# Six output parts, squares added by VectorE and other unused matmuls in a two-block fp32 kernel

## What is computed

```python
# first block
xn = rms_norm(x, attn_norm_g);  proj = xn @ w_in
x = x + concat(moba_attention(...), gated_linear_attention(...)) @ w_out
hn = rms_norm(x, ffn_norm_g)
h = causal_dwconv(hn @ w_ffn_up, conv_w, conv_b)        # width 3, over tokens
x = x + (silu(h_gate) * h_val) @ w_ffn_down             # d_ff = 2816
x = rms_norm(x, final_norm_g)
# second block: shift, scale and gate of each sublayer come from silu(c) @ w_ada + b_ada
x = x + 0.5 * g1 * swiglu(modulate(rmsnorm(x, ffn1_norm), sh1, sc1), ffn1_w_in, ffn1_w_out)
x = x + g2 * (latent attention, chunk attention, two gates, w_out)(modulate(rmsnorm(x, mix_norm), sh2, sc2))
x = x + 0.5 * g3 * swiglu(modulate(rmsnorm(x, ffn2_norm), sh3, sc3), ffn2_w_in, ffn2_w_out)
return rmsnorm(x, final_norm)
```

## Time and profile before

| | us |
|---|---|
| median of 3 runs | 876.56 |
| lowest, highest | 872.31, 880.18 |
| the profiled execution | 875.95 |
| its span (first to last instruction) | 874.1 |
| TensorE busy in it | 859.3 |

### The profile page before, as it was taken

The page is one execution under the profiler, slowest core; times in us unless marked ns, Lnnn a source line. Parts: engine busy times, 40 slices in busy tenths (PEclk is TensorE's granted clock), DMA queues, the critical chain, the costliest instruction groups (busy, mean ns, idle before and its releaser), DMA issues.

```text
span 874.1 us, 19335 instructions
## 1 busy us (share of the span) xinstructions
PE 859.3 (98%) x7326; PEld 833.8 (95%) x7326; DVE 709.1 (81%) x1109; ACT 477.7 (55%) x747; POOL 101.2 (12%) x134
## 2 busy tenths in 40 slices
PE   7999999999999999999999999999999999999996
PEld 6988899999999999999999999988999999999996
DVE  3898866889999978888889977888889998766552
ACT  4756576555555567444445567565645764444451
POOL 1031102000001540000002301000010200000021
PEclk6999999999999999999999999999999999999998
DMA  7453338566668984788889958655587568555651
GB/s 271 145 164 112 114 118 278 162 193 219 214 219 280 369 284 144 225 295 291 290 291 324 339 162 277 203 187 193 175 280 275 178 202 290 192 192 192 217 169 49
DMA packets 53384, 191.68 MB, mean 219 GB/s; under 512 B 5936, under 2 KB 6464, under 8 KB 53264
## 3 DMA queue, kind: packets, MB, share of 16 engines
q1 hardware_dynamic: 41760, 149.96, 51.3%
q0 software_dynamic: 10704, 39.20, 13.5%
q10 hardware_dynamic: 864, 1.73, 0.6%
HBM read 189.82 MB, written 1.05 MB: 218 GB/s over the span
## 4 chain that ended last, share of the span: by engine, by line
PE 91%; DVE 6%; ACT 1%; issue 1%; DMA 1%; DVEq 0%; SPq 0%; ACTq 0%
PE ps L396 27%; PE ps L397 26%; PE ps L398 26%; DVE w_lo L1320 2%; PE ps L487 1%; PE ps L489 1%; PE ps L488 1%; PE ps L563 1%; PE ps L620 1%; PE ps L509 1%; PE ps L594 1%; DVE ada_raw L1613 1%; DMA X<-x_in 1%; PE ps L580 0%; PE ps L602 0%
## 5 line engine op out<-in xcount | busy, mean ns | idle before, releaser
L1320 DVE TENSOR_TENSOR w_lo<-raw,w_hi 128x1024 fp32r<-128x1024 f32 (+1 forms) x282 | 339.8, 1221 | 76.1 <-ACT w_hi L915 75.3
L396 PE MATMUL ps<-xh,w_hi 128*128 128x256 f32 x1290 | 360.4, 279 | 0.7 <-DVE w_lo L1320 0.6
L397 PE MATMUL ps<-xl,w_hi 128*128 128x256 f32 x1290 | 357.1, 277 | 0.0
L398 PE MATMUL ps<-xh,w_lo 128*128 128x256 f32 x1290 | 357.1, 277 | 0.0
L915 ACT ACTIVATE w_hi<-raw 128x1024 fp32r<-128x1024 f32 (+1 forms) x282 | 288.6, 1050 | 94.2 <-PE ps L398 68.5
L396 PEld LDWEIGHTS ps<-xh,w_hi 128*128 128x128 f32 x1290 | 243.1, 188 | 3.7 <-issue 2.6
L397 PEld LDWEIGHTS ps<-xl,w_hi 128*128 128x128 f32 x1290 | 242.8, 188 | 0.3 <-issue 0.2
L398 PEld LDWEIGHTS ps<-xh,w_lo 128*128 128x128 f32 x1290 | 242.6, 188 | 0.0
L396 PE MATMUL ps<-act_hi,w_hi 128*128 128x256 f32 x528 | 146.6, 278 | 0.4 <-DVE act_lo L1605 0.4
L397 PE MATMUL ps<-act_lo,w_hi 128*128 128x256 f32 x528 | 146.5, 277 | 0.0
L398 PE MATMUL ps<-act_hi,w_lo 128*128 128x256 f32 x528 | 146.5, 277 | 0.0
(11 more groups left out here) (270 smaller groups left out, 1151.8 us busy)
## 6 DMA issues: line engine op xcount, KB each, us to landing
raw<-w SPq DMA_DIRECT2D x282, 512.0 KB, 4.3
ada_raw<-ada_w POOLq DMA_DIRECT2D x72, 512.0 KB, 4.9
X<-x_in SPq DMA_DIRECT2D x4, 256.0 KB, 5.4
out<-X SPq DMA_DIRECT2D x4, 256.0 KB, 2.4
tab<-tab_in ACTq DMA_DIRECT2D x1, 640.0 KB, 4.1
gmask<-gmask_in ACTq DMA_DIRECT2D x1, 512.0 KB, 5.4
cact<-c_in POOLq DMA_DIRECT2D x1, 512.0 KB, 6.5
bm<-bias_in POOLq DMA_DIRECT2D x1, 512.0 KB, 8.3
```

The lines of the kernel that those rows point to most:

```text
L396: pe.matmul(o, lh, rh, start=start, stop=False, skip_group_check=True)
L397: pe.matmul(o, lh, rl, start=False, stop=False, skip_group_check=True)
L398: return pe.matmul(o, ll, rh, start=False, stop=stop, skip_group_check=True)
L1320: v.tensor_tensor(w_lo[:, slot(h), 0:n], raw[:, slot(h), 0:n], w_hi[:, slot(h), 0:n].bitcast(F32), ALU.subtract).then_inc(lo_ready, 1)
```

## The change

- The last products go from four pairs of tiles to six parts (`LAST`: tiles 0, 1, 2 and 3, 4 and 5, 6, 7). SyncE issues the first five transfers, ScalarE the last.
- In the first norm VectorE adds squares: tiles 2 and 3 onto 0 and 1, tiles 4 and 5 onto 0 and 1, tile 7 onto 6. TensorE sums tiles 0, 1 and 6 only.
- In the first norm VectorE no longer does a low part of the weights before the reciprocal. The two low parts stand behind products 0 and 1. ScalarE converts the next weight half before the last group of `xh`.
- Unused matmuls: 6 instead of 4 at the start; 2 instead of 1 at the two entries (`IDLE_ENTRY`); two of 128 columns between sums and spread in each norm by tokens; one of 384 columns before the sums of tile 7 in the last norm.
- `first_two` waits for the first low part only before the first two products, and for the second before the others.
- In the last round of the convolved feed-forward the low part of the weights stands behind the split of the product. In the modulated feed-forwards (`raw_up`) a low part and a split of two tiles change places.

```diff
-IDLE_SPREAD = 1
+LAST = [(0, 1), (1, 1), (2, 2), (4, 2), (6, 1), (7, 1)]
+IDLE_ENTRY = {0: 2, C_UP[0]: 2}
...
-            for p in range(4):
-                sp.wait_ge(resid_done, 5 * KC + 1 + p)
-                sp.dma_start(out[:, 2 * p:2 * p + 2, :], pair(X, p)).then_inc(out_written, 16)
-            sp.wait_ge(out_written, 64)
+            for j, (k, n) in enumerate(LAST[:-1]):
+                sp.wait_ge(resid_done, 5 * KC + 1 + j)
+                sp.dma_start(out[:, k:k + n, :], X[:, k:k + n, :]).then_inc(out_written, 16)
+            sp.wait_ge(out_written, 16 * len(LAST))
...
-            def keep_clock(bank, n):
+            def keep_clock(bank, n, w=3):
                 for _ in range(n):
-                    pe.matmul(ps[:, bank, 0:3 * P], mean[:, 0, :], mean[:, :, :].rearrange("p a n -> p (a n)"), start=True, stop=True)
+                    pe.matmul(ps[:, bank, 0:w * P], mean[:, 0, :], mean[:, 0:w, :].rearrange("p a n -> p (a n)"), start=True, stop=True)
...
             def high_part_first(c, x_wait):
+                pe.wait_ge(lo_ready, 2 * c + 1)
                 pe.wait_ge(xh_ready, x_wait + 1)
                 parts = [(j, f) for j in range(2) for f in range(2)]
                 for j, f in parts:
+                    if j and f == 0:
+                        pe.wait_ge(lo_ready, 2 * c + 2)
...
-                if not shifted:
-                    keep_clock(u % 2, IDLE_SPREAD)
-                pe.wait_ge(lo_ready, h + 2)
-                if not shifted:
+                if shifted:
+                    pe.wait_ge(lo_ready, h + 2)
+                else:
+                    keep_clock(u % 2, IDLE_ENTRY[c])
                     high_part_first(c, x_wait)
...
             def norm_start():
-                for k in range(KC):
-                    if k % 2 == 0:
-                        pe.wait_ge(sq_done, k + 2)
-                    m = token_sums(k, k == 0, k == KC - 1)
+                for j, k in enumerate((0, 1, 6)):
+                    if k != 1:
+                        pe.wait_ge(first_sum, 2 if k == 0 else 3)
+                    m = token_sums(k, j == 0, j == 2)
                 m.then_inc(ss_done, 1)
                 pe.wait_ge(consts_ready, 1)
+                keep_clock(0, 2, 1)
                 norm_spread(0)
-            def norm_tokens(n, q, added, tiles_left):
+            def norm_tokens(n, q, added, tiles_left, c, ahead=0):
+                pe.wait_ge(bank_free[bank_use(c) % 2], bank_use(c) // 2)
                 for j, k in enumerate(tiles_left):
+                    if k == 7:
+                        keep_clock(bank_use(c) % 2, ahead)
...
                 m.then_inc(ss_done, 1)
+                keep_clock(bank_use(c) % 2, 2, 1)
                 norm_spread(n)
...
-            keep_clock(0, IDLE - 2)
+            keep_clock(0, IDLE)
...
-            norm_tokens(1, 1, 2, (6, 0, 1, 7))
+            norm_tokens(1, 1, 2, (6, 0, 1, 7), C_UP[0])
...
-            norm_tokens(6, 5, 24, (0, 7))
+            norm_tokens(6, 5, 24, (0, 7), C_UP[2] + FT, ahead=1)
...
-            def norm_hi(m):
+            def norm_hi(m, weights=None):
                 for j, k in enumerate(NEXT):
+                    if weights is not None and j == len(NEXT) - 1:
+                        hi(weights, halves=(0,))
...
-            norm_hi(0)
-            hi(1)
+            norm_hi(0, weights=1)
+            hi(1, halves=(1,))
...
+            k, n = LAST[-1]
+            act.wait_ge(resid_done, 5 * KC + len(LAST))
+            act.dma_start(out[:, k:k + n, :], X[:, k:k + n, :]).then_inc(out_written, 16)
...
                 rstd_tokens(n)
-                if n == 0:
-                    lo(0, halves=(1,))
                 dve.wait_ge(rstd_spread, n + 1)
                 for j, (k0, n_) in enumerate(NEXT):
...
+                    if n == 0 and j < 2:
+                        lo(0, halves=(j,))
...
-                for p in range(4):
-                    dve.wait_ge(xg_done, 2 * p + 2)
-                    v.tensor_tensor(pair(X, p), pair(xg, p), over(ps[:, 2, 0:S], 2), ALU.mult).then_inc(resid_done, 1)
+                for k, m in LAST:
+                    dve.wait_ge(xg_done, k + m)
+                    v.tensor_tensor(X[:, k:k + m, :], xg[:, k:k + m, :], over(ps[:, 2, 0:S], m), ALU.mult).then_inc(resid_done, 1)
...
-                    if j:
+                    if j and not split_first:
                         lo(c + 2, i=i, halves=(1,))
...
                 v.tensor_tensor(al, av[:, vv, :], ah.bitcast(F32), ALU.subtract).then_inc(act_ready, 1)
+                if split_first:
+                    lo(c + 2, i=i, halves=(1,))
...
-                pair_lo(m, 2)
                 lo(c0 + 4, halves=(0,))
+                pair_lo(m, 2)
...
+            for j, (a, b) in enumerate(((slice(0, 2), slice(2, 4)), (slice(0, 2), slice(4, 6)), (6, 7))):
+                dve.wait_ge(sq_done, 4 + 2 * j)
+                if j == 1:
+                    dve.wait_ge(first_sum, 1)
+                v.tensor_tensor(xn[:, a, :], xn[:, a, :], xn[:, b, :], ALU.add).then_inc(first_sum, 1)
             dve.wait_ge(cols_landed, 16)
-            lo(0, halves=(0,))
             norm_plain(0, 0, "attn_g", 1)
```

More of the change, by code:

```diff
@@ L202, in build @@
         out_written = sem("out_written")
+        first_sum = sem("first_sum")
         block = ctx.enter_context(nc.Block())
@@ L1567, in level_copy, with up_step @@
                         v.copy_predicated(dst, mask, src).then_inc(lv_copied, 1)
-            def up_step(conv, fi, c, j, i=0):
+            def up_step(conv, fi, c, j, i=0, split_first=False):
                 u = bank_use(c)
@@ L1623, in conv_up @@
                         for vv in range(2):
-                            up_step(True, 0, c0 + 2 + vv, 2 + vv, i=i)
+                            up_step(True, 0, c0 + 2 + vv, 2 + vv, i=i, split_first=n is None)
                     if n == 0:
@@ L1666, in raw_up @@
                 raw_av(fi, 1)
+                lo(c0 + 4, halves=(0,))
                 pair_lo(m, 2)
-                lo(c0 + 4, halves=(0,))
                 pair_lo(m, 3)
```

## The result

The changed kernel took 869.26 us (median of 19 runs, 868.26 to 876.60), the kernel before in the same series 874.06 us (median of 19, 870.60 to 880.32). The ratio is 0.9947, with a 95% interval of 0.9926 to 0.9968: a gain of 4.8 us, where 2.5 was forecast, and near the lower end of the range.

A forecast was written before the change was run, and what follows sets the result against it. TensorE, busy 859.3 of 874.1 us, was taken to bound the kernel outside the ends. -2.0 + 0.2 - 0.4 - 0.3 = -2.5 us gave 873.4 from the profiled execution, 874.0 by the median; range 869.0 to 878.5.

The forecast's parts named there:

- The likeliest case: Whole kernel: the forecast's gains and costs come out as summed, giving 872.5 to 875.5 us; chance 0.5.
- Start, -2.0 (0 to -3.0): First norm to gate products: shorter sums and an earlier reciprocal save 2.0 us, with 0 and 3.0 as ends.
- (a): Rival at the start, second norm and end: unused matmuls hold the clock; in all -5.4, 871.2 us; chance 0.2.
- VectorE's chain: Start: root 11.0, first product 13.1 instead of 16.09; 3.0 us won at the front become 1.7 at tile 1.
- Second norm, +0.2 (-1.3 to +0.3): 140 to 147 us: the second wide unused matmul costs 0.2 us; up to 1.3 won if the clock holds.
- Conv feed-forward, -0.4: Last round of the convolved feed-forward's loop: TensorE's stop before 273.46 us goes, saving 0.4 us, between 0.4 and 0.
- End, -0.3 (-0.7 to +0.4): Last products and output: the first transfer starts 0.27 us earlier and the end moves with it, -0.3 us.
- The swap, 0: Modulated feed-forwards: exchanging two instructions changes nothing, since TensorE doesn't stop there; 0 us.
- (b): Rival at the start: short waits for low parts keep the clock at half past 24 us; +2.5, 879.1 us; chance 0.15.
- (c): Rival for later stages: VectorE's pace or a load at its old time gives the gain back; 876.2 us; chance 0.15.

The follow-up runs named there:

- the swap alone: Kernel before, with only the low part of the weights put ahead of the split of tiles 4 and 5 in the modulated feed-forwards: 871.77 us, ratio 0.9964.
- the four output parts: Changed kernel with the last products and transfers in four pairs, all issued by SyncE: 869.31 us, ratio 0.9919 against the kernel before.
- swap undone: Changed kernel with the low part of the weights again behind the split in the modulated feed-forwards: 870.32 us, ratio 0.9965 against the kernel before.
- The squares alone: Kernel before, with VectorE adding the squares and TensorE summing only tiles 0, 1 and 6: 876.76 us, ratio 1.0001.
- one at the first entry: Changed kernel with one wide unused matmul instead of two at the first entry: 869.66 us, ratio 0.9947 against the kernel before.

## Why the prediction was right, and where it was wrong

The direction, the range and "within 1%" hold. The likeliest case doesn't: its own range was 872.5 to 875.5, and 869.26 lies 3.2 us below. Two profiles without a slow stage, the swap alone and the four output parts, split the gain: of 3.5 us of span (869.8 and 866.2) the start has 2.0 (23.44 - 21.40), the stretch to tile 1 of the second norm 1.0, since one lost its clock there and the other didn't, and all the rest 0.5. Six parts then take 0.33 back. By its steps, on low runs:

- **Start, -2.0 (0 to -3.0).** Measured -3.0 between the first two profiles and -2.1 from the middle of four to the middle of five. That the size came out is luck, for its source didn't: the 2.0 were to come from the shorter sums and the new order of VectorE, and without the added unused matmuls these gave gate products at 24.50 and a median 0.1 us under before. The step that failed is the one that priced the added unused matmuls as cost under cover. The forecast had them filling idle time and weighed their effect on the clock as rival (a), with a chance of 0.2. They are the gain. The argument against (a), that TensorE streamed from 17.17 to 21.2 at half clock, said nothing on what wide matmuls ahead of the sums do: with them the clock fell at 10.2 to 11.2 us for 3.4 us, or not at all, and without them at 7.5 to 9.8 for 10.2 to 13.7.
- **VectorE's chain.** Root, reciprocal and first product within 0.4 us of the forecast. That part of the front gain is given back was right, but it is nearly all of it: 1.74 us at the first matmul are 0.2 at the gate products when the order is changed alone, with the clock at half to 21.8.
- **Second norm, +0.2 (-1.3 to +0.3).** Measured +0.44 where the clock fell and -1.1 where it didn't, about even between the two. Both were priced; that the same code shows both wasn't foreseen, and that the added ones decide it isn't shown.
- **Conv feed-forward, -0.4.** Right: 0.46 us of stop, 0.4 and 0.65 in the medians of low runs.
- **End, -0.3 (-0.7 to +0.4).** Measured 0 for the six parts in the span and +0.33 outside it, a term that the prediction doesn't have. The failed step is "the transfer sets the end and moves with its start". The last transfer starts when the last product is done, 2.61 us after the first instead of 2.48, and its landing time doesn't depend on its size between 128 and 256 KB. The earlier first transfer had nothing to bring.
- **The swap, 0.** This is the step that was wrong in kind: "stands where TensorE doesn't stop". It stops there for 0.08 us. The stop itself is worth next to nothing, but a draw of the pace hangs on it, 6.2 us over 1392 matmuls. The swap accounts for most of what the median gained beyond the low groups' 3.3 us. The evidence by counts: with the swap undone or not made, 7 of 12, 6 of 12, 7 of 12, 4 of 9 and 53 of 118 runs of before are high; with it, none of 24 (the two kernels made from before with it) and 5 of 88 in the seven kernels of after's kind. The clean pair is the swap alone beside before; swap undone beside after (4 of 9, 3 of 19) is too few runs to stand by itself.

The rivals: (a) was right at the start and gave 871.2, by size the nearest; at the second norm it isn't decided, and at the end it failed. (b) didn't come about: the clock rose at 13.7, long before the 23.4 from which it would have decided, and the waits for low parts at 14.4 to 17.4 didn't keep it down. (c) didn't either.

What stays open: what picks the pace. The profiles show that in the long stages it is constant between waits and can change at one, in either direction, and 12 runs that a longer break without a wait didn't bring the high group back. They don't show which property of the wait decides. Nor is it shown where the change's remaining high runs (3 of 19, 2 of 12, 4 of 9) are slow, but for the two that were profiled (after and swap undone): these have it in the first feed-forward, behind a step of 0.36 us at 154.1. The squares alone went slow behind the same step, and before, the swap alone and one at the first entry have it and stayed quick.

## What to carry to other kernels

Look at the list of single runs before the median: two groups with a gap ask for another explanation than a shift, and low is to be compared with low. In a kernel bound by TensorE list every step between matmul starts that is longer than the cadence, also those too short to be marked as idle, and put the wait behind it under cover; behind a wait of 0.08 us some runs lost 6.2 us. Unused wide matmuls pay where TensorE would otherwise have only narrow or no work for some microseconds ahead of a dense stretch; they are worth testing as a gain and not to be booked as cost only. And before a difference between two profiles is put down to an edit, look how far the same stage lies apart in profiles that share its code: here by 1.3 us at the gate products, as much as most single edits were to bring.

## What the runs showed of the hardware

- **Two steady paces at the full granted clock.** Matmuls of 256 columns with a weight load each start every 113.3 or every 117.8 ns (records of 276 or 281 ns, weight loads 188 in both), for a hundred microseconds on end. The Trainium skill's page "TensorE: Matmul & The Clock Gate", section "Back-to-back issue gap", gives for a matmul without the load of weights columns over 2.4 GHz and 2.5 ns more; an estimate by it is 109.2 ns, which neither pace is.
- **The clock falls without a long idle time.** At the second norm it fell in ten of 14 profiles, at 138.4 to 144.6 us, around sums with one moving column and with TensorE idle for at most 0.55 us at a time before it. The same code at the same place lost it in some profiles and kept it in others.
- **The time for an output transfer to land** was 2.0 to 2.4 us for 128 KB and 2.3 to 2.4 for 256 KB.
- **Time outside the span.** It was 1.81 to 1.84 us (medians) for the kernels with four output transfers, all issued by SyncE, and 2.14 to 2.17 with six, the last issued by ScalarE.
